# Modulation blocks and a bias moved from TensorE to VectorE, with reordered norm and final steps, in a two-layer hybrid diffusion step on eight cores

## The chip, the cores and the metric

The kernel runs on all 8 cores of one Trainium2 chip (two dies, cores 0 to 3 and 4 to 7). Each core runs the same program on its own share of the batch; the cores don't talk to each other. The metric is the device time of the slowest core, in microseconds, as the median of several runs.

## The reference

One step of a two-layer trunk, for context and latent tokens of width 1024. Each layer norms and modulates, mixes tokens, norms and modulates again, and runs an MLP with a squared ReLU:

```python
for l in range(DEPTH):                                   # 2 layers
    mod = (jax.nn.silu(cond) @ ada_w[l] + ada_b[l])[:, None, :]
    sh_m, sc_m, g_m, sh_f, sc_f, g_f = jnp.split(mod, N_MOD, axis=-1)
    h = rmsnorm(x, norm_mix_g[l]) * (1.0 + sc_m) + sh_m
    y = even_mixer(h, ...) if l % 2 == 0 else odd_mixer(h, ...)
    x = x + g_m * y
    h = rmsnorm(x, norm_ffn_g[l]) * (1.0 + sc_f) + sh_f
    x = x + g_f * (jnp.square(jax.nn.relu(h @ ffn_w1[l])) @ ffn_w2[l])
return rmsnorm(x, final_norm_g), outs_f, outs_b
```

`cond` is one vector for all context tokens and one per request for the latent tokens, so a core needs `mod` for two vectors. The even mixer is a chunked gated linear attention with a Fourier group; the odd one has a gated MLP over chunks of 128 positions and a short convolution:

```python
u, v = jnp.split(jax.nn.gelu(uv), 2, axis=-1)
sp = jnp.einsum('gpq,bnqgc->bnpgc', ws, vc) + bs.T[:, :, None]   # the gating bias
out_c = u * sp.reshape(bsz, L, GMLP_WIDTH)
out_d = gb * conv3(gc * hin, conv_w)
return jnp.concatenate([out_c, out_d], axis=-1) @ w_out
```

## The kernel before

**Tiles.** A core has 1536 tokens in three blocks `m` of 512, taken in the order MO = (2, 0, 1). Activations lie transposed: eight chunks of 128 channels in the partitions, tokens along the free axis. `xT[m]` holds the residual stream in f32, `hT` the modulated norm in bf16. A matmul group (`group`, L327) is 8 or 16 matmuls of 128x128 weights by 512 tokens into one PSUM bank; `PS()` (L285) hands out six banks in turn, and a second pair serves the sums of squares.

**Order of work.** Each engine runs its instructions in the order in which the program emits them; `Tracker.op` (L89) adds semaphore waits for the operands. Two lists mix work into the stream of groups. `defer` (L295) holds matmuls of the sums of squares, run some groups later by `pe_tick`. `side` holds the steps of a norm: `side_pop` (L313), called at the end of each `group`, emits `rate[0]` of them, before the consumer of that group's bank. `norm_steps` (L568) gives one step for the reciprocal root (Ln and Exp on ScalarE, into the one buffer `rstd`) and eight steps `ap(c)`: a product on VectorE into `ntm[c % 2]`, then at once the Identity with the shift on ScalarE that reads it. `norm_end` (L591) empties `side`, emits the root, and queues the steps; `need(m)` (L599) empties what is left before a block is read.

**Ada blocks.** `mod` is computed in twelve blocks of 1024 outputs. `ada_block` (L444) takes 64 weight loads of 128x128 with 64 matmuls of two columns, and one small addition on VectorE. Five run in the first half of the kernel; seven (`ada_next` in `ffn`) run in the MLP of layer 0, one after each w1 or w2 block of weights but the last.

**Weights.** Three slots of 2 MB (128 x 8192 bf16) take all weights in the order of `WSEQ`, in turn; `wpump` (L394) issues the next load on POOL's queue when its slot is free, and stops at the first that is not. `wdone` frees a slot.

**MLP** (`ffn`, L683). In each of two halves: two w1 blocks with 24 groups of eight matmuls (ReLU on ScalarE into one of two `relu_t`, square on VectorE), then two w2 blocks with 12 groups of sixteen matmuls (residual on VectorE, `resid` L606). In the last w2 block squares and norms run beside the groups; at the end of the kernel `final_steps` (L580) and `final_parts` (L632) do the last norm, for the last block of tokens in parts of 320 and 192 columns, and store the output.

**Gating** (`gmlp`, L1372). Per 128 tokens: one matmul of 33 rows by 512 columns puts the bias into the bank, four matmuls of 128 columns accumulate onto it, and VectorE multiplies with `uT`. Seven calls lie in the loop over the V groups, five in the output projection.

Helpers record their operations under one line each: L319 matmul, L333 activation, L336 tensor-tensor, L339 scalar-tensor-tensor (STT), L115 DMA.

Of the kernel before, what the change touches and what calls it, by code (L numbers as in the profile page):

```python
# [193 lines left out]
def build():  # L194
# [30 lines left out]
    with contextlib.ExitStack() as es:
# [25 lines left out]
        att = [sb("att%d" % i, [128, 512], BF16) for i in range(2)]  # L251
# [3 lines left out]
        relu_t = [sb("relu%d" % i, [128, 512], BF16) for i in range(2)]  # L255
# [99 lines left out]

        WSEQ = []
# [17 lines left out]
        for l in range(2):  # L374
# [3 lines left out]
            late = [(0, 5)] + [(1, k) for k in range(6)] if l == 0 else []  # L378
# [9 lines left out]
        wslot = [early[j] if j < len(early) else (2, 0, 1)[(j - len(early)) % 3] for j in range(len(WSEQ))]  # L388
        hw_b = Buf("hwslot")
        wstate = dict(issued=0, hold=len(early))  # L390
        wused = set()
        occ = [None] * NSLOT

        def wpump():  # L394
            while wstate["issued"] < min(len(WSEQ), wstate["hold"]):
                j = wstate["issued"]
                nm, n, src = WSEQ[j]
                sl = wslot[j]
                if occ[sl] is not None:
                    break  # L400
                occ[sl] = j
# [1088 lines left out]
```

How the kernel before makes its waits and increments, by code:

```python
    def _emit(self, e, need, fn):  # L71
        items = list(need.items())
        for key, (sem, val) in items[:-1]:
            e["h"].wait_ge(sem, val)
            e["seen"][key] = val
        ins = fn()
        if items:
            key, (sem, val) = items[-1]
            ins._wait_ge(sem, val)
            e["seen"][key] = val
        return ins
# [7 lines left out]
    def op(self, ek, fn, reads=(), writes=(), sig=True):  # L89
# [2 lines left out]
        e = self.eng[ek]  # L92
        need = self._collect(e, reads, writes)
        ins = self._emit(e, need, fn)
        if sig:
            e["cnt"] += 1
            ins.then_inc(e["sem"], 1)
            val = e["cnt"]
        else:
# [25 lines left out]
    def barrier(self, engines=("pe", "act", "dve", "sp")):  # L125
        if self.dead:
            return
        targets = [(k, e["sem"], e["cnt"]) for k, e in self.eng.items() if e["cnt"] > 0]
        targets += [("dma%d" % b.id, b.dsem, b.dcnt) for b in self.owners if b.dcnt > 0]
        for ek in engines:
            e = self.eng[ek]
            for key, sem, val in targets:
                if key == ek and ek == "pe":
                    continue
                if e["seen"].get(key, 0) >= val:
                    continue
                e["h"].wait_ge(sem, val)
                e["seen"][key] = val
# [1 line left out]
    def wait_all(self, ek, bufs):  # L140
        e = self.eng[ek]
        need = self._collect(e, [], bufs)
        for key, (sem, val) in need.items():
            e["h"].wait_ge(sem, val)
            e["seen"][key] = val
```

## Time and profile before

| | us |
|---|---|
| median of 3 runs | 1162.25 (1160.67 to 1163.19) |
| the profiled execution | 1162.37 |
| its span, slowest core (4) | 1161.1 |
| VectorE busy | 463.2 (40%) |
| ScalarE busy | 430.6 (37%) |
| POOL busy | 151.8 (13%) |

The span runs from the first to the last instruction of a core; the time of the execution has the launch on top. Busy time of TensorE overlaps itself, since matmuls are pipelined and their ends are modelled: one matmul of 512 columns is listed with 379 ns, while the starts of two in a row may lie closer. How fast TensorE goes is therefore read from start to start. A row of a timeline has its start, its duration from the first start to the last end, engine, line, operation, output and inputs, how many instructions are merged in it, and in brackets the idle time before it with what ended it.

### The profile page before, as it was taken

The page shows a single profiled execution, that of the slowest core. Times are in us where ns is not written, and L with a number is a line of the kernel's source. Part 1 is how long each engine was busy: PE and PEld are TensorE (multiplying, and loading weights), DVE is VectorE, ACT ScalarE, POOL GpSimd, SP SyncE. Part 2 cuts the span into 40 slices and gives each one's busy share as a digit, 9 for nine tenths or more (in the row PEclk, how much of TensorE's full clock was granted, in tenths as well). Part 3 has the DMA queues.
Part 4 walks back from the last instruction along what each step waited for, and adds up shares of the span by engine and source line. Part 5 has one row for each costly group of instructions (what it writes and reads, how often), then busy time and mean ns, then how long its engine had stood idle before and what let it go on. Part 6 is the DMA issues. An engine that isn't in the chain of part 4 may idle for free.

```text
span 1161.1 us, 16258 instructions; the slowest of 8 cores (1157.7 to 1161.1 us)
## 1 busy us (share of the span) xinstructions
PE 1094.6 (94%) x6519; PEld 547.6 (47%) x6519; DVE 463.2 (40%) x839; ACT 430.6 (37%) x823; POOL 151.8 (13%) x185
## 2 busy tenths in 40 slices
PE   2589999989999999999999999999999999999995
PEld 0234777755434444444444444444344444444444
DVE  2134588885642222222222637547432222222227
ACT  2275788856653200133202721227543000332032
POOL 1100223433400000000003300024000000000030
PEclk9998999999999999999999999999999999999999
DMA  9953747445367368458456224440440441240005
GB/s 183 215 120 63 124 79 167 87 153 115 64 113 123 68 101 127 73 91 133 69 90 109 36 37 73 73 73 1 73 73 5 69 73 28 46 73 1 1 1 218
DMA packets 14859, 99.27 MB, mean 85 GB/s; under 512 B 1578, under 2 KB 6858, under 8 KB 8768
## 3 DMA queue, kind: packets, MB, share of 16 engines
q0 software_dynamic: 6992, 81.07, 40.8%
q1 hardware_dynamic: 7248, 16.77, 4.4%
q8 instruction: 51, 0.84, 0.3%
q10 hardware_dynamic: 544, 0.39, 0.1%
q14 instruction: 24, 0.20, 0.1%
HBM read 164.88 MB, written 7.86 MB: 149 GB/s over the span
## 4 chain that ended last, share of the span: by engine, by line
PE 80%; ACT 8%; DVE 7%; DMA 3%; issue 2%; POOL 0%; ACTq 0%; DVEq 0%; POOLq 0%
PE psf L319 79%; DMA sb_slot<-evC 3%; DVE sb_ntm L339 2%; DVE sb_X L339 2%; ACT sb_hT L333 2%; ACT sb_relu L333 1%; ACT sb_A L333 1%; ACT sb_B L333 1%; DVE sb_A L336 1%; ACT sb_rstd L333 1%; ACT sb_lnr L333 1%; DVE sb_X L336 0%; PE psf L1058 0%; DVE sb_A L339 0%; ACT sb_X L347 0%
## 5 line engine op out<-in xcount | busy, mean ns | idle before, releaser
L319 PE MATMUL psf<-sb_hT,sb_slot 128*128 128x512 bf16 (+1 forms) x2472 | 557.9, 383 | 12.5 <-ACT sb_relu L333 4.9
L319 PEld LDWEIGHTS psf<-sb_hT,sb_slot 128*128 128x128 bf16 (+1 forms) x2472 | 240.1, 98 | 309.1 <-issue 15.0
L319 PE MATMUL psf<-sb_A,sb_slot 128*128 128x512 bf16 (+2 forms) x1696 | 359.4, 371 | 0.0
L319 PEld LDWEIGHTS psf<-sb_A,sb_slot 128*128 128x128 bf16 x1696 | 164.8, 98 | 186.8
L333 ACT ACTIVATE sb_relu<-psf 128x512 bf16<-128x512 f32 x192 | 113.6, 595 | 351.1 <-PE psf L319 350.0
L339 DVE SCALAR_TENSOR_TENSOR sb_X<-psf,sb_modT,sb_X 128x512 f32<-128x512 f32 (+2 forms) x148 | 108.4, 734 | 256.0 <-PE psf L319 255.9
L336 DVE TENSOR_TENSOR sb_A<-sb_relu 128x512 bf16<-128x512 bf16 x192 | 81.7, 425 | 237.4 <-ACT sb_relu L333 237.0
L333 ACT ACTIVATE sb_B<-sb_X 128x512 bf16<-128x512 f32 (+2 forms) x100 | 57.8, 607 | 155.0 <-DVE sb_X L339 145.7
L319 PE MATMUL psf<-sb_slot,sb_hT 128*128 128x192 bf16 (+2 forms) x672 | 90.5, 289 | 2.0 <-DVE sb_B L339 1.6
L508 POOL TENSOR_TENSOR sb_B<-sb_B 128x512 f32<-128x512 bf16 (+2 forms) x48 | 56.8, 1191 | 168.6 <-ACT sb_B L333 159.9
L333 ACT ACTIVATE sb_A<-psf 128x192 bf16<-128x192 f32 (+2 forms) x98 | 45.4, 466 | 78.3 <-PE psf L319 76.2
L319 PEld LDWEIGHTS psf<-sb_slot,sb_hT 128*128 128x128 bf16 x672 | 58.8, 98 | 26.1 <-ACT sb_A L333 1.3
L339 DVE SCALAR_TENSOR_TENSOR sb_ntm<-sb_X,sb_gscT,sb_rstd 128x512 f32<-128x512 f32 x72 | 58.7, 826 | 22.1 <-ACT sb_rstd L333 21.0
L333 ACT ACTIVATE sb_hT<-sb_ntm,sb_modT 128x512 bf16<-128x512 f32 x72 | 51.4, 721 | 38.3 <-DVE sb_ntm L339 38.0
L349 DVE CAST sb_A<-psf 128x512 bf16<-128x512 f32 (+1 forms) x33 | 22.2, 687 | 61.0 <-PE psf L319 61.0
L115 POOL DMA_DIRECT2D sb_slot<-w x16 | 8.6, 538 | 276.0 <-PE psf L319 276.0
L319 PE MATMUL psf<-sb_scT,sb_slot 128*128 128x2 bf16 x768 | 21.1, 163 | 21.0 <-DMA sb_slot<-adaw 21.0
L115 POOL DMA_DIRECT2D sb_slot<-adaw x12 | 6.6, 548 | 260.6 <-PE psf L319 260.6
L319 PE MATMUL psf<-sb_B,sb_onesb 128*128 128x512 bf16 (+2 forms) x53 | 19.1, 398 | 17.1 <-ACT sb_B L333 16.0
L319 PEld LDWEIGHTS psf<-sb_scT,sb_slot 128*128 128x128 bf16 x768 | 21.0, 97 | 23.3 <-DMA sb_slot<-adaw 21.6
L336 DVE TENSOR_TENSOR sb_X<-sb_X,sb_rstd 128x512 f32<-128x512 f32 (+1 forms) x30 | 19.1, 690 | 21.8 <-ACT sb_rstd L333 21.6
L508 POOL TENSOR_TENSOR sb_A<-sb_A 128x512 f32<-128x512 bf16 (+2 forms) x18 | 21.2, 1177 | 34.1 <-ACT sb_A L333 34.1
(125 smaller groups left out, 614.2 us busy)
## 6 DMA issues: line engine op xcount, KB each, us to landing
sb_slot<-w POOLq DMA_DIRECT2D x16, 2048.0 KB, 17.4
sb_slot<-adaw POOLq DMA_DIRECT2D x12, 2048.0 KB, 17.0
sb_X<-xT SPq DMA_DIRECT2D x6, 1024.0 KB, 10.3
sb_X<-xT POOLq DMA_DIRECT2D x4, 1024.0 KB, 29.1
yT<-sb_X SPq DMA_DIRECT2D x8, 512.0 KB, 3.3
sb_X<-xT POOLq DMA_DIRECT2D x4, 512.0 KB, 9.3
sb_slot<-evH POOLq DMA_DIRECT2D x1, 2048.0 KB, 16.7
sb_slot<-dft SPq DMA_DIRECT2D x1, 2048.0 KB, 17.2
```

The costliest lines, as they stand in the source:

```text
L115: ins = self._emit(e, need, lambda: e["h"].dma_start(out=out, in_=in_))
L319: T.op("pe", lambda: nc.tensor.matmul(out, l, r, start=start, stop=stop), reads=R, writes=W, sig=stop if sig is None else sig)
L333: T.op("act", lambda: nc.scalar.activation(out=out, in_=in_, func=func, **kw), reads=R, writes=W)
L336: T.op("dve", lambda: nc.vector.tensor_tensor(out=out, in0=a, in1=b, op=op), reads=R, writes=W)
L339: T.op("dve", lambda: nc.vector.scalar_tensor_tensor(out=out, in0=a, scalar=scalar, in1=b, op0=op0, op1=op1), reads=R, writes=W)
L349: T.op("dve", lambda: nc.vector.tensor_copy(out, in_), reads=R, writes=W)
L508: T.op("pool", lambda: nc.gpsimd.tensor_tensor(out=o[0], in0=a[0], in1=b[0], op=ALU.add), reads=[a[1], b[1]], writes=[o[1]])
```

## The change

Eight edits in one. Five ada blocks, (0,5), (1,0), (1,1), (1,2) in the MLP of layer 0 and (1,5) in that of layer 1, are computed on VectorE: the host lays their weights out with outputs in the partitions, the two Silu vectors are broadcast to all partitions (a load of 1 MB on SP's queue and two activations, in each MLP), and sixteen STT of 1024 columns with an accumulated sum give the block. A counter of units, one per w1 group and two per w2 group, places them: one per unit, from unit 17 + 28 i on. Blocks (1,3) and (1,4) stay on TensorE, later than before. The list of slots is written out by hand, and `wpump` no longer stops at a slot that is taken but goes on to loads for other slots. The norm's Identity of chunk c - 1 is emitted ahead of the product of chunk c, in nine steps for eight. In the final norm the roots of the later blocks go to `ntm[0]` and `ntm[1]` in place of `rstd`; in `final_parts` the side steps are emitted behind the residual and the square of a group, not ahead of them. The gating bias is computed once by a matmul, copied to SBUF in f32 (over `relu_t`), and added on VectorE, into `ntm`, before the product with `uT`.

```diff
+        ON_PE = ((1, 3), (1, 4))
+        LATE = ([(0, 5), (1, 0), (1, 1), (1, 2), (1, 3), (1, 4)], [(1, 5)])
...
-        wslot = [early[j] if j < len(early) else (2, 0, 1)[(j - len(early)) % 3] for j in range(len(WSEQ))]
+        wslot = list(early)
+        late_slots = [2, 0, 1, 0, 2, 0, 1, 0, 2, 0, 1, 0, 2, 1, 2, 1, 0, 2, 1, 2, 0, 1, 0, 1, 0, 1, 0]
+        wslot += late_slots[:len(WSEQ) - len(wslot)]
+        assert len(wslot) == len(WSEQ), (len(wslot), len(WSEQ))
...
         def wpump():
-            while wstate["issued"] < min(len(WSEQ), wstate["hold"]):
-                j = wstate["issued"]
+            blocked = set()
+            for j in range(min(len(WSEQ), wstate["hold"])):
+                sl = wslot[j]
+                if j in issued or sl in blocked:
+                    continue
+                if occ[sl] is not None:
+                    blocked.add(sl)
+                    continue
+                occ[sl] = j
                 nm, n, src = WSEQ[j]
...
+        def final_steps(m):
+            rf, rfb = (rstd, rstd_b) if m == MO[0] else (ntm[0], ntm_b[0])
+
+            def rs_():
+                ps, pb = sbank[m]
+                act(lnr[:], ps[:], AF.Ln, [pb, on_b], [lnr_b], bias=cst[:, 0:1])
+                act(rf[:], lnr[:], AF.Exp, [lnr_b], [rfb], scale=-0.5)
...
             def ap(c):
-                stt(ntm[c % 2][:], xT[m][:, c, :], gscT[l][:, wh, c, ci:ci + 1], rstd[:], ALU.mult, ALU.mult,
-                    [xT_b[m][c], rstd_b, gsc_b[l][wh]], [ntm_b[c % 2]])
-                act(hT[:, c, msl(m)], ntm[c % 2][:], AF.Identity, [ntm_b[c % 2], mod_b[l][shb]], [hT_b[m][c]],
-                    bias=modT[l][:, shb * 8 + c, ci:ci + 1])
-
...
+                if c > 0:
+                    act(hT[:, c - 1, msl(m)], ntm[(c - 1) % 2][:], AF.Identity, [ntm_b[(c - 1) % 2], mod_b[l][shb]], [hT_b[m][c - 1]],
+                        bias=modT[l][:, shb * 8 + c - 1, ci:ci + 1])
+                if c < 8:
+                    stt(ntm[c % 2][:], xT[m][:, c, :], gscT[l][:, wh, c, ci:ci + 1], rstd[:], ALU.mult, ALU.mult,
+                        [xT_b[m][c], rstd_b, gsc_b[l][wh]], [ntm_b[c % 2]])
+
+            return [lambda: rstd_calc(m)] + [lambda c=c: ap(c) for c in range(9)]
...
-                    act(rstd[:, hs], lnr[:, hs], AF.Exp, [st["l"]], [st["r"]], scale=-0.5)
+                    act(ntm[1][:, hs], lnr[:, hs], AF.Exp, [st["l"]], [st["r"]], scale=-0.5)
...
-                rate[0] = 2 + hh
+                rate[0] = 0
...
                     qdefer(1, s_, fn)
+                    side_pop(2 + hh)
...
+        def sc_rows(olds):
+            stg = B[:, 0:4096].bitcast(F32)
+            sb_ = ab("stg", olds)
+            T.dma("sp", stg, condb_d, Buf("condb"), writes=[sb_])
+            sc = ab("scB", att_b + olds)
+
+            def silu(k):
+                act(scB[k], stg[:, k * 1024:(k + 1) * 1024], AF.Silu, [sb_], [sc])
...
+        def ada_rows(l, b, sc, jk):
+            st = {}
+
+            def one(oc, k):
+                if not st:
+                    st["s"], st["b"] = wget("ada%d_%d" % (l, b))
+                w = st["s"][:, oc * 1024:(oc + 1) * 1024]
+                T.op("dve", lambda: nc.vector.scalar_tensor_tensor(out=B[:, 1024 * k:1024 * (k + 1)], in0=w, scalar=1.0, in1=scB[k],
+                                                                   op0=ALU.mult, op1=ALU.mult, accum_out=mraw[:, oc, k:k + 1]),
+                     reads=[st["b"], sc], writes=[jk[k], mraw_b])
+                if oc == 7 and k == 1:
+                    wdone(st["b"])
+                    mod_add(l, b, mraw[:], mraw_b)
+
+            return [lambda oc=oc, k=k: one(oc, k) for oc in range(8) for k in range(2)]
...
+            sc, jk, silu = sc_rows(B_all)
+            B_all.extend([sc] + jk)
+            rows = {14: [lambda: silu(0), lambda: silu(1)]}
+            for i, (la, ba_) in enumerate([x for x in LATE[l] if x not in ON_PE]):
+                for k_, fn in enumerate(ada_rows(la, ba_, sc, jk)):
+                    rows.setdefault(17 + 28 * i + k_, []).append(fn)
+            late = [x for x in LATE[l] if x in ON_PE]
+            un = [0]
+
+            def unit(n):
+                for _ in range(n):
+                    for fn in rows.get(un[0], []):
+                        fn()
+                    un[0] += 1
 
...
                             tt(aT[:, ch, msl(m)], relu_t[i][:], relu_t[i][:], ALU.mult, [relu_b[i]], [aT_b[ch][m]])
+                            unit(1)
                     wdone(slb)
-                    ada_next()
+                    if hf == 1 and b == 1 and late:
+                        ada_block(*late.pop(0))
...
                             resid(l, 5, oc, m, ps, pb)
+                            unit(2)
...
-                    if not last:
-                        ada_next()
+                    if pre and late:
+                        ada_block(*late.pop(0))
...
+        biasf = relu_all[:].bitcast(F32)
+        bias_b = ab("bias", relu_b)
+        ps, pb = PS()
+        mm(ps[:], ones33[:], gb33[:], [on_b, gb_b], [pb])
+        cp(biasf, ps[:], [pb], [bias_b], "dve")
...
-            mm(ps[:], ones33[:], gb33[:], [on_b, gb_b], [pb], start=True, stop=False)
             for g in range(4):
-                mm(ps[:, g * 128:(g + 1) * 128], v1[:, j, g * 128:(g + 1) * 128], wsT(g), [v1_b[j], wst_b], [pb],
-                   start=False, stop=(g == 3))
-            tt(hT[:, 0:4, tsl(j)], ps[:].rearrange("p (g t) -> p g t", g=4), uT[:, :, tsl(j)], ALU.mult,
-               [pb] + [u_b[c][m] for c in range(4)], [hT_b[m][c] for c in range(4)])
+                mm(ps[:, g * 128:(g + 1) * 128], v1[:, j, g * 128:(g + 1) * 128], wsT(g), [v1_b[j], wst_b], [pb], sig=(g == 3))
+            nt, ntb = ntm[j % 2], ntm_b[j % 2]
+            tt(nt[:], ps[:], biasf, ALU.add, [pb, bias_b], [ntb])
+            tt(hT[:, 0:4, tsl(j)], nt[:].rearrange("p (g t) -> p g t", g=4), uT[:, :, tsl(j)], ALU.mult,
+               [ntb] + [u_b[c][m] for c in range(4)], [hT_b[m][c] for c in range(4)])
```

On the host, `adaw` keeps its old layout for the seven blocks that stay on TensorE and is transposed for the five others; `condb` is the pair of conditioning vectors, repeated over 128 partitions. `mod_add` is the addition at the end of `ada_block`, made a function.

## Rows read from the trace of the kernel before

**Rows 1.** The cores: span, mean granted clock of TensorE.

```profile
core 0: 1157.8 us, clock 0.993
...
core 4: 1161.1 us, clock 0.991
```

**Rows 2.** Busy time, share of the span and instructions, from the page.

```profile
PE 1094.6 (94%) x6519; PEld 547.6 (47%) x6519; DVE 463.2 (40%) x839; ACT 430.6 (37%) x823; POOL 151.8 (13%) x185
```

**Rows 3.** Timeline of the first MLP's first groups, 317 to 340 us.

```profile
317.70 9.23 PE L319 MATMUL psf<-sb_hT,sb_slot 128*128 128x512 bf16 x42
...
327.24 1.90 PE L319 MATMUL psf<-sb_hT,sb_slot 128*128 128x512 bf16 x8 [0.31 <-ACT sb_relu L333]
...
329.92 0.75 DVE L339 SCALAR_TENSOR_TENSOR sb_ntm<-sb_X,sb_gscT,sb_rstd 128x512 f32<-128x512 f32 x1
330.70 0.72 ACT L333 ACTIVATE sb_hT<-sb_ntm,sb_modT 128x512 bf16<-128x512 f32 x1 [1.16 <-DVE sb_ntm L339]
331.33 0.58 ACT L333 ACTIVATE sb_relu<-psf 128x512 bf16<-128x512 f32 x1
331.94 0.42 DVE L336 TENSOR_TENSOR sb_A<-sb_relu 128x512 bf16<-128x512 bf16 x1 [1.27 <-ACT sb_relu L333]
...
339.04 13.99 PE L319 MATMUL psf<-sb_hT,sb_slot 128*128 128x512 bf16 x64 [0.46 <-ACT sb_relu L333]
```

**Rows 4.** Timeline of the second MLP's first groups, TensorE, 819 to 842 us.

```profile
819.73 11.90 PE L319 MATMUL psf<-sb_hT,sb_slot 128*128 128x512 bf16 x53
...
832.09 1.90 PE L319 MATMUL psf<-sb_hT,sb_slot 128*128 128x512 bf16 x8 [0.46 <-ACT sb_relu L333]
...
841.53 1.69 PE L319 MATMUL psf<-sb_hT,sb_slot 128*128 128x512 bf16 x7 [0.46 <-ACT sb_relu L333]
```

**Rows 5.** Timeline of TensorE around one ada block, 352 to 355 us.

```profile
352.86 1.74 PE L319 MATMUL psf<-sb_scT,sb_slot 128*128 128x2 bf16 x64
...
354.46 3.83 PE L319 MATMUL psf<-sb_hT,sb_slot 128*128 128x512 bf16 x17
```

**Rows 6.** Timeline of TensorE in the V loop with gating, 749 to 753 us.

```profile
749.67 0.39 PE L319 MATMUL psf<-sb_gb,sb_ones 33*128 33x512 bf16 x1
...
749.99 0.40 PE L319 MATMUL psf<-sb_cb,sb_A 128*128 128x128 bf16 x4
...
750.23 1.89 PE L319 MATMUL psf<-sb_slot,sb_hT 128*128 128x512 bf16 x8
...
752.05 0.39 PE L319 MATMUL psf<-sb_gb,sb_ones 33*128 33x512 bf16 x1
```

**Rows 7.** VectorE by shape: busy us, mean ns of one, idle before.

```profile
L339 DVE SCALAR_TENSOR_TENSOR sb_X<-psf,sb_modT,sb_X 128x512 f32<-128x512 f32 x140 | 104.6, 749 | 255.9 <-PE psf L319 255.9
...
L339 DVE SCALAR_TENSOR_TENSOR sb_A<-sb_B,sb_pp,sb_A 128x1008 f32<-128x1008 f32 x8 | 10.1, 1268 | 0.3
```

**Rows 8.** ScalarE by shape, same columns.

```profile
L333 ACT ACT_TABLE_LOAD x10 | 12.8, 1283 | 15.2 <-PE psf L319 14.0 <-PEq L195 1.1
...
L333 ACT ACTIVATION_READ_ACCUMULATOR sb_A<-psf 128x1 f32 x48 | 9.4, 196 | 0.0
```

**Rows 9.** The tail from 1129 us: TensorE's waits (us, times, longest), then timeline.

```profile
PE psf L319 <- ACT sb_B L333: 3.8, 3, 1.5
...
1138.27 0.63 ACT L333 ACTIVATE sb_rstd<-sb_lnr 128x512 f32<-128x512 f32 x1 [1.23 <-DVE sb_X L339]
...
1153.92 2.72 DVE L339 SCALAR_TENSOR_TENSOR sb_X<-sb_X,sb_pp,sb_rstd 128x192 f32<-128x192 f32 x8 [1.59 <-ACT sb_rstd L333]
```

**Rows 10.** The loads of ada blocks, twelve of 2 MB, from issue to landing.

```profile
DMA to landing us min/median/max: 16.4/17.0/34.2
```

**Rows 11.** Windows of core 4: TensorE busy (instructions), granted clock, DMA share, GB/s.

```profile
290.00:295.00 5.00, 5.00 (x20) 0.81 0.96 177
...
850.00:1130.00 280.00, 280.00 (x1299) 1.00 0.22 38
```

More of the change, by code:

```diff
@@ L250, in build @@
         lnr_b = Buf("lnr")
-        att = [sb("att%d" % i, [128, 512], BF16) for i in range(2)]
+        att_all = sb("att", [128, 1024], BF16)
+        att = [att_all[:, i * 512:(i + 1) * 512] for i in range(2)]
+        mraw = sb("mraw", [128, 8, 2])
         att_b = [Buf("att0"), Buf("att1")]
@@ L254, in build @@
         ntm_b = [Buf("ntm0"), Buf("ntm1")]
-        relu_t = [sb("relu%d" % i, [128, 512], BF16) for i in range(2)]
+        relu_all = sb("relu", [128, 1024], BF16)
+        relu_t = [relu_all[:, i * 512:(i + 1) * 512] for i in range(2)]
         relu_b = [Buf("relu0"), Buf("relu1")]
@@ L377, in build @@
                 wadd("odUV", 8192, odUV_d); wadd("odO", 8192, odO_d)
-            late = [(0, 5)] + [(1, k) for k in range(6)] if l == 0 else []
+            late = LATE[l][:]
             for hf in range(2):
@@ L405, in wpump @@
                     T.dma("pool", slots[sl][:, 0:n], src, slot_b[sl], writes=[slot_b[sl]])
-                wstate["issued"] += 1
+                issued.add(j)
+                blocked.add(sl)
         def wget(name):
             j = [i for i in range(len(WSEQ)) if WSEQ[i][0] == name and i not in wused][0]
-            assert wstate["issued"] > j, name
+            assert j in issued, name
             wused.add(j)
@@ L681, in final_parts @@
                 side.pop(0)()
+        scB = [att_all[:], B[:, 7168:8192]]
+        mraw_b = Buf("mraw")
+        def sc_rows(olds):
[5 more added lines that the diff above has]
+                act(scB[k], stg[:, k * 1024:(k + 1) * 1024], AF.Silu, [sb_], [sc])
+                if k == 1:
+                    for j in jk:
+                        for dct in (sb_.w, sb_.r):
+                            for key, (sem, val) in dct.items():
+                                Tracker._rec(j.r, key, sem, val)
+            jk = [ab("jk", olds) for _ in range(2)]
+            return sc, jk, silu
+        def ada_rows(l, b, sc, jk):
[11 more added lines that the diff above has]
+            return [lambda oc=oc, k=k: one(oc, k) for oc in range(8) for k in range(2)]
         def ffn(l, nxt):
@@ L688, in ffn @@
             k = [0]
-            late = [(0, 5)] + [(1, k) for k in range(6)] if l == 0 else []
-            def ada_next():
-                if late:
-                    ada_block(*late.pop(0))
+            sc, jk, silu = sc_rows(B_all)
[11 more added lines that the diff above has]
+                    un[0] += 1
             rate[0] = 1
@@ L1401, in build @@
                     gmlp(rest.pop(0))
+        for b in relu_b:
+            for dct in (bias_b.w, bias_b.r):
+                for key, (sem, val) in dct.items():
+                    Tracker._rec(b.r, key, sem, val)
         ffn(1, "final")
```

38 lines of the change are left out of this document (20 added, 18 removed).

## Prediction

> **What bounds the kernel now.** I read the spans of all cores first: core 4 takes 1161.1 us, core 0 takes 1157.8 us, and the granted clock is 0.991 and 0.993 [rows 1]. The slowest core sets the time, so all the work below is on core 4. The share of busy time names TensorE: 1094.6 us of the span [rows 2]. Busy is not yet bound, so I looked at the pitch. Between 339.04 and 352.86 us TensorE starts 64 matmuls of 512 columns, 13.82 us or 0.216 us each [rows 3, 5]; one group of eight is 1.73 us. Most of both MLPs runs at that pitch, so there an instruction less on TensorE is time less, and VectorE and ScalarE have room. The exceptions are found in the chain of waits, which leaves TensorE in the norm before either MLP and again in the last 30 us; the timelines of those stretches show where.
>
> First exception: in the first MLP, groups start 2.36 us apart ((339.04 - 327.24) / 5) [rows 3]. The rows between show the ring: VectorE's norm product (0.75 us), ScalarE's Identity that waits for it, ScalarE's ReLU queued behind that Identity, and VectorE's square that waits for the ReLU and stands ahead of the next product [rows 3]. Together they take 2.36 us where TensorE needs 1.73. Second exception: at the end TensorE waits 3.8 us for ScalarE's squares, and VectorE's queue is full of final products [rows 9].
>
> **Ada blocks.** Five of twelve blocks leave TensorE. One block delays the next group from 352.86 to 354.46 us: 1.60 us [rows 5], although its weight loads and matmuls number 64 each. Five: **8.0 us**. (Its modelled busy time, 1.74 us, would give 8.7; I take the pitch.)
>
> What they add to VectorE: 16 products of 128x1024 per block, each with an accumulated sum. No row shows that form. The nearest is the 128x1008 product at 1.27 us [rows 7]; ScalarE's accumulator read is a separate 0.20 us [rows 8]. So I take 1.45 us. The lower end is 0.6 us (two products of 512 would run 1.5 us, and two bf16 elements per cycle, as the square seems to do at 0.42 us [rows 3] against 0.75, would halve that); the upper end is twice the row, 2.5 us. They are spread one to a unit, a unit being one w1 group or half a w2 group. In a w1 unit VectorE then has 0.42 + 1.45 = 1.87 us against 1.73: it falls behind by 0.14 us a unit, 2.2 us over 16 units, and has 12 empty units after each block to catch up. The cover is the ring of six PSUM banks: TensorE may run five groups ahead, 5 x 1.73 = 8.6 us, before VectorE's lag reaches it through the ReLU. In w2 groups it is 0.75 [rows 7] + 2.90 = 3.65 us against 3.45, with twice the cover. Cost nothing, as long as the cover holds; it fails in w1 units from 16 x (0.42 + x - 1.73) = 8.6, that is x = 1.85 us. Behind a waiting product on VectorE stand the square, and behind it ReLU and the bank.
>
> Each of the two MLPs also gets a 1 MB load of the conditioning rows on SP's queue (nothing needed soon is behind it; it shares the engines with a weight load when TensorE has its weights already), two Silu of 1024 columns and a table load at unit 14. A 512-column Identity is 0.72 us [rows 3], so two Silu are at most 2.9 us, with 1.28 us for the table [rows 8]: 4.2 us, against 8.6 us of cover and after the norm is through. Going back to Ln costs 1.28 us once more in each final norm; in the second MLP that lies on the tail and is counted there.
>
> **Slots.** A slot is now held through 16 units, and weights are loaded by slot, not in one order. The tightest pair is the second block: its load can start when the first is read out (unit 33, some 2 us late) and it is needed at unit 45, 12 x 1.73 = 20.7 us later; landing takes 17.0 us in the middle and 34.2 at worst [rows 10]. Cover: the same 8.6 us. The w1 and w2 weights keep 24 units, 41 us. On POOL's queue each load waits behind nothing later than itself. Cost nothing.
>
> **Gating bias.** One turn of the V loop takes 752.05 - 749.67 = 2.38 us; its V group is 1.73 and its four gating matmuls 750.23 - 749.99 = 0.24 [rows 6]. The bias matmul with its weight load thus costs 0.41 us, more than its 0.216 us of columns. Twelve go, one comes: 11 x 0.41 = **4.5 us** (by columns alone 2.4, the lower end; 4.9 the upper). VectorE gets 12 additions and a copy of 0.7 us, against 1.97 us of TensorE per turn: hidden.
>
> **Norm skew.** With the Identity of c - 1 ahead of the product of c, ScalarE never waits for the product just issued. VectorE then has 0.75 + 0.42 and ScalarE 0.72 + 0.60 us per group, both under 1.73. In the first MLP the 42 matmuls from 317.70 should have ended at 326.8, and the next start at 327.24 is 0.5 us late; five turns lose 0.63 each: 3.7 us [rows 3]. In the second, 53 matmuls from 819.73 end at 831.2, the next starts at 832.09 (0.9 late), four turns follow to 841.53 and lose 2.5: 3.5 us [rows 4]. Together **7.2 us**, if the stall goes wholly; the upper end is that, the lower zero. The flush before the last rstd remains, some 4 us of lag on ScalarE (three Identities and rstd) which the banks cover.
>
> **Tail.** Residuals come ahead of the final products, and the Exp no longer waits for the old products (1.23 us at 1138.27) [rows 9]. But VectorE's own work fills most of the tail, and the 8 products of 192 columns after the last rstd stay (2.72 us from 1153.92) [rows 9], so at most the 3.8 us of TensorE's waits come back; the table load (1.28 us) may come on top. I take **1.5 us**, between -1.3 and 3.8.
>
> **Sum.** 8.0 + 4.5 + 7.2 + 1.5 = 21.2 us. The profiled execution took 1162.4 us (span and launch), 0.1 above the median: 1162.4 - 21.2 - 0.1 = **1141.1 us**.
>
> **Rivals.** (1) The norm stall stays in another form, with the extra step of ten instead of nine before need() or with the flush: 1141.1 + 7.2 = 1148.3. For it: the flush puts three steps and both root activations on ScalarE at once. Against: both engines have 0.4 us to spare per group.
> (2) VectorE's accumulating product is dearer, 2.0 us: each of the three blocks in w1 units (two in the first MLP, one in the second) stalls TensorE by 16 x 0.69 - 8.6 = 2.4 us: 7.3 in all, 1148.4.
> (3) **Slower**: the product costs double, 2.5 us. Then each of the three w1 blocks stalls 16 x 1.19 - 8.6 = 10.4 us and the w2 blocks 1 us each, 33 us in all: 1174. It turns slower than before from x = 2.29 us, where 3 x (16 x (x - 1.31) - 8.6) passes 21. Against it: the product with two f32 operands from SBUF runs 0.75 us, just as the one with a PSUM operand [rows 3, 7].
> The Trainium skill (Vector Engine (DVE) Microarchitecture Reference, section 7, Points that are easy to get wrong) says that a scalar-tensor-tensor with two non-bf16 SBUF sources halves throughput for want of a port for the accumulator. The trace shows no halving without an accumulator, and the new sources are bf16, so by its own words the rule spares this change; were it to hold here, it would be this rival.
> (4) The clock: with fewer gaps the granted clock falls. It was 0.81 for 5 us at 290 us on core 4, and 1.00 (2.4 GHz) through 850 to 1130 us where TensorE had no gap at all [rows 11]. At 0.81 the 21 us are used up after some 90 us. One sentence of the Trainium skill bears on it: TensorE: Matmul & The Clock Gate, Part 1, has the whole die fall to 13/16 once three cores run dense matmuls, for as long as they do; eight cores ran dense for 280 us here without it, so the trace disagrees.
> (5) The edits do not do what they say: the blocks moved are on TensorE's path by the row, so only a misplaced slot could undo them; I give it nothing of its own.
>
> **Chances.** Forecast 0.76; (1) 0.09; (2) 0.08; (3) 0.04; (4) 0.03. A measurement tells 0.2% (2.3 us) from no change. All but (3) and (4) are faster by more: 0.93, and of the rest 0.02 the same and 0.05 slower. The range: best ends 8.7 + 4.9 + 7.2 + 3.8 = 24.6 give 1137.6, and the 1.5 us that core 4 lost to the clock dip may be absent, 1136; at the top it takes in (1) and (2), 1150.
>
> **What would show it.** The idle-before of ReLU-bound matmuls gone at 325 and 830 us; groups 1.73 us apart through both; 448 instead of 768 ada matmuls; VectorE's new rows near 1.45 us and no PE wait behind them; V turns at 1.97 us; a tail of 2 us less. What would make it wrong: the new products over 1.85 us, a DMA wait on VectorE over 8 us, or a clock below 1.00 in the MLPs.

## The result, and the profile after

The changed kernel takes 1145.43 us (median; 1143.69 to 1146.15) where the kernel before, run beside it, takes 1161.83 us: a ratio of 0.9854, with an interval of 0.9837 to 0.9871. That is 16.4 us less by the medians (17.0 by the ratio), inside the range of the prediction (1136 to 1150) and 4.3 us above its point. Now and then one die runs slow for a long stretch of an execution (one of the four of the changed kernel took 1245.22 us, with one die at a mean clock of 0.90, and with the mended tail below it went down to 0.81); such executions are left out of the ranges and ratios but not of the medians, which puts 1145.43 where 1144.9 would stand and moves no other median given below by more than 0.4 us. In a second comparison on another chip, told below, the same kernel takes 1140.67 us against 1160.23.

The spans of all cores come first. These are those of the profiled execution of the changed kernel (1146.15 us):

```profile
core 3: 1144.7 us, clock 0.986
core 4: 1138.5 us, clock 0.993
...
die 0 (median of its cores): 1143.7 us, clock 0.988
die 1 (median of its cores): 1138.5 us, clock 0.993
```

The program is the same on all cores, yet one die is 5.2 us longer, at a lower clock. The windows of core 3 show where (TensorE busy, weight loads, VectorE, ScalarE, POOL, granted clock, DMA share, GB/s):

```profile
290.00:300.00 10.00, 10.00 (x42) 4.23 (x40) 8.25 (x12) 6.43 (x11) 4.68 (x4) 0.86 1.05 203
...
760.00:770.00 10.00, 10.00 (x50) 4.62 (x49) 7.10 (x12) 3.15 (x5) 5.20 (x5) 0.91 0.65 109
810.00:820.00 10.00, 10.00 (x43) 4.28 (x42) 5.90 (x12) 6.88 (x12) 0.00 (x0) 0.88 0.89 159
850.00:1130.00 280.00, 279.33 (x1342) 130.50 (x1341) 80.27 (x143) 57.53 (x97) 16.52 (x17) 1.00 0.27 52
```

The clock sags for ten microseconds at a time at several places and is 1.00 on the mean from 850 us on. It is the same kind of dip as in [rows 11], only more of them. To see what the edits did I therefore compare cores without a dip: core 0 of before (1157.8 us, clock 0.993 [rows 1]) and core 4 of after (1138.5 us, 0.993). The starts of the 192 ReLUs of both MLPs cut either span into stretches:

| stretch | before | after | difference |
|---|---|---|---|
| start to the first ReLU | 308.86 | 308.94 | +0.1 |
| MLP of layer 0, first 48 w1 groups | 84.99 | 80.07 | -4.9 |
| its w2 groups | 89.41 | 84.60 | -4.8 |
| next 48 w1 groups | 82.75 | 81.16 | -1.6 |
| last w2 groups and the odd mixer | 244.51 | 239.78 | -4.7 |
| MLP of layer 1, first 48 w1 groups | 83.32 | 80.19 | -3.1 |
| its w2 and w1 groups | 165.76 | 165.75 | 0.0 |
| last ReLU to the end | 98.2 | 98.0 | -0.2 |
| span | 1157.8 | 1138.5 | -19.3 |

The page after, beside [rows 2]: VectorE has 100.6 us more work, TensorE 331 matmuls less, five blocks of 64 and 11 for the bias.

```profile
PE 1083.2 (95%) x6188; PEld 541.0 (47%) x6188; DVE 563.8 (49%) x1012; ACT 437.2 (38%) x831; POOL 153.2 (13%) x185
```

The first MLP on TensorE, core 4, beside [rows 3], and then the second, beside [rows 4]. The columns are start, duration, engine, line, operation, output and inputs, how many:

```profile
310.99 34.26 PE L323 MATMUL psf<-sb_hT,sb_slot 128*128 128x512 bf16 x158
```

```profile
799.74 45.49 PE L323 MATMUL psf<-sb_hT,sb_slot 128*128 128x512 bf16 x210
```

Each is one unbroken row, where before there were gaps that ended with a ReLU. The timeline of core 4 shows the conditioning rows being made, and then the units with an accumulating product:

```profile
332.64 1.28 ACT L337 ACT_TABLE_LOAD   x1
...
333.94 1.06 ACT L337 ACTIVATE sb_att<-sb_B 128x1024 bf16<-128x1024 f32 x1
335.02 1.06 ACT L337 ACTIVATE sb_B<-sb_B 128x1024 bf16<-128x1024 f32 x1
...
339.56 0.42 DVE L340 TENSOR_TENSOR sb_A<-sb_relu 128x512 bf16<-128x512 bf16 x1
339.90 1.22 DVE L738 SCALAR_TENSOR_TENSOR sb_B<-sb_slot,sb_B 128x1024 bf16<-128x1024 bf16 x1
...
341.05 0.08 DVE L738 DVE_READ_ACCUMULATOR sb_B<-sb_slot,sb_B 128x1 f32 x1
341.29 0.43 DVE L340 TENSOR_TENSOR sb_A<-sb_relu 128x512 bf16<-128x512 bf16 x1 [0.16 <-ACT sb_relu L337]
```

From the square at 339.56 to the end of the accumulator's read at 341.13 VectorE needs 1.57 us, and then it idles 0.16 us for the next ReLU: a unit costs less than the group's 1.73. By shape (busy us, mean ns of one, idle before), core 4, with ScalarE's table loads under it:

```profile
L738 DVE SCALAR_TENSOR_TENSOR sb_B<-sb_slot,sb_att 128x1024 bf16<-128x1024 bf16 x40 | 48.8, 1220 | 0.5
L738 DVE SCALAR_TENSOR_TENSOR sb_B<-sb_slot,sb_B 128x1024 bf16<-128x1024 bf16 x40 | 48.7, 1217 | 0.0
...
L337 ACT ACT_TABLE_LOAD x14 | 18.0, 1283 | 15.2 <-PE psf L323 14.0 <-PEq L195 1.1
```

The V loop with gating on TensorE, core 4, beside [rows 6]:

```profile
741.62 0.39 PE L323 MATMUL psf<-sb_cb,sb_A 128*128 128x128 bf16 x4
741.84 1.89 PE L323 MATMUL psf<-sb_slot,sb_hT 128*128 128x512 bf16 x8
743.57 0.39 PE L323 MATMUL psf<-sb_cb,sb_A 128*128 128x128 bf16 x4
```

A turn is 743.57 - 741.62 = 1.95 us, where it was 2.38. And the tail, core 4, beside [rows 9]:

```profile
1112.92 0.55 DVE L343 SCALAR_TENSOR_TENSOR sb_X<-psf,sb_modT,sb_X 128x320 f32<-128x320 f32 x1 [1.36 <-PE psf L323]
...
1113.38 3.92 DVE L343 SCALAR_TENSOR_TENSOR sb_X<-sb_X,sb_pp,sb_rstd 128x512 f32<-128x512 f32 x5
...
1117.22 0.54 DVE L343 SCALAR_TENSOR_TENSOR sb_X<-psf,sb_modT,sb_X 128x320 f32<-128x320 f32 x1
...
1126.22 1.01 DVE L343 SCALAR_TENSOR_TENSOR sb_X<-sb_X,sb_pp,sb_ntm 128x320 f32<-128x320 f32 x2 [1.46 <-ACT sb_ntm L337]
1127.15 0.41 DVE L343 SCALAR_TENSOR_TENSOR sb_X<-psf,sb_modT,sb_X 128x192 f32<-128x192 f32 x1
...
1130.87 2.72 DVE L343 SCALAR_TENSOR_TENSOR sb_X<-sb_X,sb_pp,sb_ntm 128x192 f32<-128x192 f32 x8 [0.21 <-ACT sb_ntm L337]
```

VectorE idles 1.36 us at 1111.56, with five old products at hand that it is only given at 1113.38; these hold the next residual back until 1117.22. Near the end it waits 1.46 us for the second root, and the residual at 1127.15 stands behind the two products that need that root. The order of the tail is new, and its work is a little shorter: the last eight products start 20.33 us after the first 320-column part (1110.54), where that was 21.01. Of these 0.7 us the table shows only 0.2, because the span goes on for 4.9 us behind the last product (which ends at 1133.59), where that was 4.4; only stores and semaphore instructions lie there.

### The profile page after: what moved, and what is told of

Its sections match the earlier page's. It is cut to its first block, busy times and chain, and to the rows that moved or that the text cites. A ratio compares the mean times of both kernels' runs of the same rounds, so it can differ in the third digit from the quotient of the medians.

```text
span 1144.7 us, 15757 instructions; the slowest of 8 cores (1137.1 to 1144.7 us)
## 1 busy us (share of the span) xinstructions
PE 1083.2 (95%) x6188; PEld 541.0 (47%) x6188; DVE 563.8 (49%) x1012; ACT 437.2 (38%) x831; POOL 153.2 (13%) x185
## 4 chain that ended last, share of the span: by engine, by line
PE 86%; ACT 5%; DVE 4%; DMA 3%; issue 1%; POOL 0%; ACTq 0%; DVEq 0%; POOLq 0%
PE psf L323 85%; DMA sb_slot<-evC 3%; DVE sb_X L343 2%; ACT sb_B L337 1%; ACT sb_A L337 1%; ACT sb_hT L337 1%; DVE sb_A L340 0%; ACT sb_lnr L337 0%; DVE sb_X L340 0%; PE psf L1134 0%; ACT sb_rstd L337 0%; DVE sb_A L343 0%; DVE sb_ntm L343 0%; ACT sb_X L351 0%; ACT L337 0%
## 5 line engine op out<-in xcount | busy, mean ns | idle before, releaser
L738 DVE SCALAR_TENSOR_TENSOR sb_B<-sb_slot,sb_att 128x1024 bf16<-128x1024 bf16 x40 | 48.8, 1220 | 0.5
L738 DVE SCALAR_TENSOR_TENSOR sb_B<-sb_slot,sb_B 128x1024 bf16<-128x1024 bf16 x40 | 48.7, 1217 | 0.0
L323 PE MATMUL psf<-sb_B,sb_onesb 128*128 128x512 bf16 (+2 forms) x53 | 19.3, 403 | 15.9 <-ACT sb_B L337 15.0
L323 PE MATMUL psf<-sb_scT,sb_slot 128*128 128x2 bf16 x448 | 12.4, 164 | 22.3 <-DMA sb_slot<-adaw 22.3
L526 POOL TENSOR_TENSOR sb_A<-sb_A 128x512 f32<-128x512 bf16 (+2 forms) x18 | 21.2, 1176 | 33.8 <-ACT sb_A L337 33.8
```

Of the source, the lines that this page charges most:

```text
L323: T.op("pe", lambda: nc.tensor.matmul(out, l, r, start=start, stop=stop), reads=R, writes=W, sig=stop if sig is None else sig)
L526: T.op("pool", lambda: nc.gpsimd.tensor_tensor(out=o[0], in0=a[0], in1=b[0], op=ALU.add), reads=[a[1], b[1]], writes=[o[1]])
L738: T.op("dve", lambda: nc.vector.scalar_tensor_tensor(out=B[:, 1024 * k:1024 * (k + 1)], in0=w, scalar=1.0, in1=scB[k], op0=ALU.mult, op1=A ...
```

## The experiments

**The four parts alone.** Four kernels each have one part of the change, all else as before, run on one chip beside the kernel before (1159.78 us).

Only the ada blocks with their slots and `wpump`:

```diff
+        ON_PE = ((1, 3), (1, 4))
+        LATE = ([(0, 5), (1, 0), (1, 1), (1, 2), (1, 3), (1, 4)], [(1, 5)])
+            sc, jk, silu = sc_rows(B_all)
```

> Kernel before with the ada edit alone: five blocks on VectorE, the new list of slots, the loads by slot; norm order, tail and bias as before. Theory (work leaves TensorE's path at its pitch): each core 8.0 us (5 x 1.60) shorter than the kernel before on an undisturbed die, the norm stall of 2.36 us per group still there before both MLPs. Rival (the moved work costs something on VectorE or through the slots): less than 6 us. On the clock: if the denser matmul stream makes the clock dip, the dips on the disturbed die grow here by 1 to 2 us; if the norm order does it, they stay as in the kernel before.

Measured: 1152.41 us, 7.4 less, ratio 0.9939 (0.9923 to 0.9955). The ReLU stall of [rows 3] is still there; TensorE's waits, core 4 (us, times, longest):

```profile
PE psf L323 <- ACT sb_relu L337: 4.9, 11, 0.5
```

The stretches hold the full 8.0 us (first w1 groups 84.99 to 83.38, w2 groups 89.41 to 84.61, next w1 groups 82.75 to 81.15). But from the last ReLU to the end it is 98.6 us on all cores for 98.2, although the tail is untouched: the last product ends where it did, and the part behind it is 0.4 us longer. Why is open.

Only the skewed norm steps:

```diff
+                if c > 0:
+                    act(hT[:, c - 1, msl(m)], ntm[(c - 1) % 2][:], AF.Identity, [ntm_b[(c - 1) % 2], mod_b[l][shb]], [hT_b[m][c - 1]],
+                        bias=modT[l][:, shb * 8 + c - 1, ci:ci + 1])
...
+            return [lambda: rstd_calc(m)] + [lambda c=c: ap(c) for c in range(9)]
```

> Kernel before with the norm order alone (Identity of chunk c - 1 ahead of the product of chunk c). Theory: TensorE's waits for ReLU before both MLPs vanish, 6.4 us shorter (3.3 in the first MLP, 3.1 in the second, as the milestones of the changed kernel give), groups 1.73 us apart throughout. Rival: part of the 6.4 us came from the other edits and less than 4 us is seen here. On the clock: if taking gaps from TensorE in stretches with all engines busy brings dips, the disturbed die gives 2 us or more of it back.

Measured: 1152.57 us, 7.2 less, ratio 0.9943 (0.9925 to 0.9961). No wait of TensorE for a ReLU is left. On core 0 the first 48 w1 groups go from 84.99 to 81.66 us, 3.3 less, those of layer 1 from 83.32 to 80.19, 3.1 less, and the stretch with the odd mixer from 244.51 to 244.18.

Only the gating bias on VectorE:

```diff
+        cp(biasf, ps[:], [pb], [bias_b], "dve")
...
+            tt(nt[:], ps[:], biasf, ALU.add, [pb, bias_b], [ntb])
```

> Kernel before with the gating bias on VectorE alone. Theory: the bias matmul with its exposed weight load costs 0.41 us a turn, so 4.5 us shorter (4.7 by the milestones of the changed kernel). Rival (a bias matmul costs only its 512 columns, 0.216 us): 2.4 us.

Measured: 1155.75 us, 4.0 less, ratio 0.9965 (0.9952 to 0.9978). On core 4 the stretch with the odd mixer goes from 244.51 to 239.83 us, 4.7 less, as in the whole change.

Only the tail:

```diff
-                rate[0] = 2 + hh
+                rate[0] = 0
...
+                    side_pop(2 + hh)
```

> Kernel before with the tail edit alone: own root buffers, residual and square ahead of the side steps in the last parts. The changed kernel's last ReLU to its end took 98.0 us against 98.2 before, so the forecast 1.5 us was not there. Theory 1 (the edit itself gives nothing, because VectorE idles 1.4 us at the first part and the root of part one comes 1 us later): 0 to 0.7 us shorter here too. Theory 2 (the edit gives 1.5 us and the table load of 1.28 us took it back): 1.3 to 1.5 us shorter here, where no table load lies ahead of the last norm.

Measured: 1159.03 us, 0.75 less, ratio 0.9991 (0.9981 to 1.0001): by the times no difference that can be told from none. The traces do tell one: from the last ReLU to the end it is 97.4 to 97.5 us on all eight cores, where it was 98.2.

The four add up: 7.4 + 7.2 + 4.0 + 0.75 = 19.4 us.

**The changed kernel again**, unaltered, on another chip beside before (1160.23 us). The question is whether the longer die of the first comparison belongs to the program.

> The changed kernel itself, once more. The four parts alone gave 7.4, 7.2, 4.0 and 0.8 us, 19.4 in sum. Theory 1 (the parts add up; the 3 us that were missing in the first comparison are clock dips of one die, which belong to the execution): 19 us shorter here if both dies are undisturbed, with all cores alike within 2 us and the clock near 0.993. Theory 2 (the four together load the chip so that one die's clock dips more than with any part alone): cores of one die 4 to 6 us longer than the other again, at 0.987 or so, and 15 to 16 us shorter in all.

Measured: 1140.67 us, 19.6 less, ratio 0.983 (0.982 to 0.9841). The dies of its profiled execution:

```profile
die 0 (median of its cores): 1138.5 us, clock 0.993
die 1 (median of its cores): 1138.3 us, clock 0.992
```

Both are as core 4 was in the first comparison. The parts lose nothing when they are put together (19.4 against 19.6), and the 5 us of one die are the clock's in those executions: the same program runs without them here. The chip of the first comparison was not tried again, so whether the dips belong to that chip or to that series was not found out.

**The tail mended.** In the final norm the old steps are no longer emptied at once, the root is emitted without waiting for a turn, and two products go ahead of the first part's first residual, where VectorE idled.

```diff
-            while side:
+            while side and nxt != "final":
...
-                side.append(rs_)
+                rs_()
...
+                    if hh == 0 and o == 0:
+                        side_pop(2)
...
-                    side_pop(2 + hh)
+                    side_pop(2)
```

> The changed kernel with another tail: the old steps of the final norm are no longer emptied ahead of the next root, the root of each last part is emitted at once and not through the side list, two side steps go ahead of the first part's residual, and two instead of three behind each residual of the second. Theory (VectorE's idle time of 1.4 us at the first part and of 1.5 us before each late root is what the tail edit left): last ReLU to end falls from 98.0 to about 96 us, 2 us shorter than the changed kernel. Rival (the tail is set by TensorE's own groups and the last chain of residual, square, sum, root and products): under 0.5 us.

Measured: ratio to before 0.9816 (0.9792 to 0.984); two executions, 1138.28 and 1139.43 us. The dies are at 1136.3 and 1136.5 us, 2.0 less than in the run above, but only 1.3 of it lies in the tail: on core 4 the last ReLU to the end falls from 98.0 to 96.7 us, where about 96 was expected. Of TensorE's 3.2 us of waits for ScalarE in the tail this is left on core 4:

```profile
PE psf L323 <- ACT sb_B L337: 0.6, 1, 0.6
```

So the tail held some 1.3 us that the change didn't take. Which of the four edits gives how much of it was not taken apart.

**A sixth block.** On top of the mended tail, block (1,3) goes to VectorE too, the blocks 27 units apart instead of 28 so that all five of layer 0's MLP are read out before its last w1 group, unit 143.

```diff
-        ON_PE = ((1, 3), (1, 4))
+        ON_PE = ((1, 4),)
-                    rows.setdefault(17 + 28 * i + k_, []).append(fn)
+                    rows.setdefault(17 + 27 * i + k_, []).append(fn)
```

> The kernel with the other tail, and a sixth ada block, (1,3), on VectorE in the MLP of layer 0, with blocks 27 units apart in place of 28. Theory (each block is worth 1.60 us of TensorE's pitch while VectorE keeps up): 1.6 us shorter than with five. Rival (the load of the next block has 11 units, 19 us, against a landing of 18, and VectorE's wait for it reaches TensorE): no gain or a loss, with TensorE waiting for ReLU.

Measured: 1137.55 us, ratio 0.9804 (0.9787 to 0.9821). The stretch that holds block (1,3) goes from 239.79 (the mended tail) to 238.18 us: 1.6, the price of a block once more. The dies:

```profile
die 0 (median of its cores): 1135.0 us, clock 0.993
die 1 (median of its cores): 1134.4 us, clock 0.992
```

The loop of loads told of below has 27 x 1.73 = 46.7 us here. This is the fastest version of the study, 3.1 us under the changed kernel by the medians of one chip.

**The accumulating product twice.** This measures the cover: what TensorE feels once VectorE falls behind.

```diff
+                for _ in range(2):
+                    T.op("dve", lambda: nc.vector.scalar_tensor_tensor(out=B[:, 1024 * k:1024 * (k + 1)], in0=w, scalar=1.0, in1=scB[k],
+                                                                       op0=ALU.mult, op1=ALU.mult, accum_out=mraw[:, oc, k:k + 1]),
+                         reads=[st["b"], sc], writes=[jk[k], mraw_b])
```

> The changed kernel with each accumulating product issued twice, so that a unit has 2.6 us of it (measured 1.22 + 0.08 each). This puts rival 3 of the prediction to the test. By its formula each of the three blocks in w1 units stalls TensorE by 16 x (0.42 + 2.6 - 1.73) - 8.6 = 12.0 us and the two in w2 units by 8 x (0.75 + 5.2 - 3.45) - 17.2 = 2.8 us: 42 us longer than the changed kernel, 22 us longer than the kernel before. If the banks cover more than five groups (two ReLU buffers on top), 6 to 10 us less than that. If VectorE's lag is hidden otherwise, no change.

Measured: 1191.75 us, ratio 1.027 (1.0245 to 1.0294): 51 us over the changed kernel, 9 more than expected. VectorE in the first block, core 0:

```profile
352.43 0.42 DVE L340 TENSOR_TENSOR sb_A<-sb_relu 128x512 bf16<-128x512 bf16 x1
...
354.03 1.23 DVE L739 SCALAR_TENSOR_TENSOR sb_B<-sb_slot,sb_att 128x1024 bf16<-128x1024 bf16 x1
...
355.18 0.42 DVE L340 TENSOR_TENSOR sb_A<-sb_relu 128x512 bf16<-128x512 bf16 x1
```

A unit is 2.75 us, so over 16 units VectorE falls 16 x (2.75 - 1.73) = 16.4 us behind. The first 48 w1 groups on core 0 grow from 80.06 to 86.65 us, by 6.6; the second MLP's by the same (86.73 against 80.19). The cover is thus 16.4 - 6.6 = 9.8 us. But the other stretches grow more: the w2 groups by 10.8 and the next w1 groups by 21.9 us (103.05 against 81.15), and there VectorE waits for its weights:

```profile
DVE sb_B L739 <- DMA sb_slot<-adaw: 21.4, 3, 10.8
```

The load of the next block waits for the read-out of the last, and the one behind it on POOL's queue waits along (TensorE did not wait for that one here). POOL, core 0:

```profile
440.07 0.53 POOL L115 DMA_DIRECT2D sb_slot<-adaw  x1 [45.73 <-DVE sb_modT L340]
440.58 0.54 POOL L115 DMA_DIRECT2D sb_slot<-w  x1
```

**One short product more.** A product of 512 columns is added to each accumulating one (its result isn't used). This is rival (2) made real.

```diff
+                stt(B[:, 1024 * k:1024 * k + 512], w[:, 0:512], 1.0, scB[k][:, 0:512], ALU.mult, ALU.mult, [st["b"], sc], [jk[k]])
```

> The changed kernel with one more product of 512 columns beside each accumulating product (its result is not used), so that a unit has about 2.0 us of them: rival 2 of the prediction. By the prediction's formula each of the three blocks in w1 units stalls TensorE by 16 x (0.42 + 2.0 - 1.73) - 8.6 = 2.4 us, 7.3 us in all. Theory from the run with doubled products: there the pitch of VectorE was 2.75 us a unit, 16.4 us of lag over the first block, and TensorE lost 6.6 us, so the cover is 9.8 us; here the pitch is about 2.1 us, 6 us of lag, all of it covered: no change against the changed kernel (within 0.5 us).

Measured: 1148.61 us in the middle of three executions (1147.86 to 1150.11), ratio to before 0.9899 (0.9878 to 0.992), 8 us over the changed kernel. The cores fall into two groups:

```profile
core 0: 1138.4 us, clock 0.993
core 1: 1147.8 us, clock 0.991
...
core 3: 1148.7 us, clock 0.993
```

A unit now takes VectorE 2.21 us on either core (squares at 346.70 and 348.91 us on core 0), 0.48 more than a group, or 7.7 us behind per block, inside the cover of 9.8. And on both the first 48 w1 groups take what they took, 80.06 and 80.07 us. The 9 us between the cores come later: in the next w1 groups core 1 takes 88.87 us and core 0 81.33. The issues of the ada loads on POOL, core 0 and then core 1:

```profile
373.58 0.53 POOL L115 DMA_DIRECT2D sb_slot<-adaw  x1 [25.33 <-DVE sb_modT L340]
423.22 0.53 POOL L115 DMA_DIRECT2D sb_slot<-adaw  x1 [33.53 <-DVE sb_modT L340]
472.14 0.53 POOL L115 DMA_DIRECT2D sb_slot<-adaw  x1 [41.01 <-DVE sb_modT L340]
520.88 0.53 POOL L115 DMA_DIRECT2D sb_slot<-adaw  x1 [47.69 <-DVE sb_modT L340]
```

```profile
375.19 0.53 POOL L115 DMA_DIRECT2D sb_slot<-adaw  x1 [25.33 <-DVE sb_modT L340]
426.14 0.53 POOL L115 DMA_DIRECT2D sb_slot<-adaw  x1 [34.85 <-DVE sb_modT L340]
477.74 0.53 POOL L115 DMA_DIRECT2D sb_slot<-adaw  x1 [45.01 <-DVE sb_modT L340]
530.03 0.53 POOL L115 DMA_DIRECT2D sb_slot<-adaw  x1 [51.23 <-DVE sb_modT L340]
```

And the landings of all twelve ada loads, core 0 and then core 1:

```profile
DMA to landing us min/median/max: 12.6/14.9/34.3
```

```profile
DMA to landing us min/median/max: 15.3/17.0/35.3
```

The issues are 49.6, 48.9 and 48.7 us apart on core 0, and 51.0, 51.6 and 52.3 us on core 1. The blocks are placed 28 units apart, 28 x 1.73 = 48.4 us. But a block's load can only be issued when the block before is read out, then it must land, and then it is read out in 16 units: a closed loop. The read-out takes 16 x 2.21 = 35.4 us. The loads behind the first three issues shown land after 14.0, 13.3 and 13.3 us on core 0 and after 15.3, 16.0 and 16.9 us on core 1, so the loop should take 49.4, 48.7 and 48.7 us on core 0 and 50.7, 51.4 and 52.3 on core 1: the distances of the issues to within 0.3 us. Where the loop is longer than the 48.4 us, each turn puts VectorE further behind, and the cover is spent once, not given anew to each block. On core 1 VectorE waits for these loads:

```profile
DVE sb_B L343 <- DMA sb_slot<-adaw: 17.8, 3, 9.5
```

On core 0 it waits 5.2 us for them. The other cores go the same way: on four of the eight the ada loads land after 14.9 to 16.4 us in the median, and the next w1 groups take 81.3 to 83.0 us; on the other four it is 16.9 to 17.3 us, and they take 88.9 to 91.3.

The doubled kernel fits: 17.0 + 16 x 2.75 = 61.0 us, and on its core 1 the issues are 60.9, 62.3 and 60.7 us apart. In the changed kernel the loop takes 17.0 + 16 x 1.73 = 44.7 us, with 3.7 us to spare. Why an ada load lands 2 us sooner on some cores is open. In each of the three executions one core of each pair of neighbours (0 and 1, 2 and 3, 4 and 5, 6 and 7) is short, 1137 to 1141 us, and the other long, 1146 to 1149 us; which of the two it is changes between executions, so neither the core's data nor its place decides it.

**The doubled kernel with its blocks 36 units apart**, so that the loop (61.0 us) fits into 36 x 1.73 = 62.3.

```diff
-                    rows.setdefault(17 + 28 * i + k_, []).append(fn)
+                    rows.setdefault(17 + 36 * i + k_, []).append(fn)
```

> The changed kernel with doubled products, blocks 36 units apart in place of 28. Theory (of the 51 us that doubling cost at 28 units, VectorE's lag against the banks makes 6.6 us for each block in w1 units, and the rest comes from loads that start late because the slot is read out late, with VectorE waiting 21 us for them): with 8 more units between blocks those waits go, and the cost falls from 51 to 15 to 25 us over the changed kernel. Rival (all of it is VectorE's own work against the cover, slots play no part): it stays above 40 us.

Measured: 1194.02 us, ratio 1.0293 (1.0277 to 1.031): no gain, where 15 to 25 us were expected. VectorE no longer waits for an ada load on core 0, where that was 21.4 us. But the fourth block is now read out about where the w1 groups end, and the slot that it holds is the one that block (1,3) needs, which runs on TensorE right behind them. TensorE, core 0:

```profile
559.63 7.93 PE L323 MATMUL psf<-sb_hT,sb_slot 128*128 128x512 bf16 x34
...
595.65 1.84 PE L323 MATMUL psf<-sb_scT,sb_slot 128*128 128x2 bf16 x64 [28.09 <-DMA sb_slot<-adaw]
```

Its load is issued at 581.43 us. The wait moved from VectorE to TensorE, by my placing of the blocks. The w2 groups, 10.8 us longer in the doubled kernel, are 1.4 us longer here (86.04 us against 84.61, core 0), with 23 units of products among them for 29. So this run confirms that the spacing takes the loop's wait from VectorE; the forecast of the total failed, and what the total would be without a late load is not shown.

## Why the prediction came out as it did

**What bounds.** Right: work taken from TensorE in the MLPs and the V loop came back as time, one for one, on all the cores that no dip disturbed.

**Ada blocks, 8.0 us.** Right: three blocks less in the w2 stretch give 4.8 us, one in the next w1 stretch 1.6, one in the first w1 stretch 1.6 (84.99 to 83.38 in the kernel with this edit alone), and the sixth block 1.6. That kernel gained 7.4 and not 8.0 us; 0.4 of the difference is the longer end behind the last product, a term that the prediction doesn't have. The pitch of [rows 5] was the right row, not the busy time. The product was taken at 1.45 us and costs 1.23 (339.90 to 341.13), with its accumulator's read at 0.08 us against ScalarE's 0.20 [rows 8]. Thus VectorE doesn't fall behind by 0.14 us a unit but has 0.16 to spare. The cover of 8.6 us measured 9.8. The two Silu of 1024 columns take 2.1 us and the table 1.3, under the bound of 4.2, and TensorE shows no gap there.

**Slots, nothing.** Right in this kernel, but the reasoning had a hole that the runs with a dearer product laid open. I put the pair's 20.7 us against a landing of 17.0 and then gave it "the same 8.6 us" of cover, as if each pair began anew. The loads form a loop: lag adds up from turn to turn. The loop breaks at a unit of (48.4 - 17.0) / 16 = 1.96 us (at 2.19 with the 13.3 us of core 0, which a unit of 2.21 hardly hurt), the banks of a single block only at 1.73 + 9.8 / 16 = 2.34 us. The threshold in the prediction, 1.85 us a product or 2.27 a unit, stood for the banks alone; the loads come first. "On POOL's queue each load waits behind nothing later than itself" also failed: once VectorE is late, a weight load is queued behind the ada load that waits for VectorE (440.07 us above).

**Gating bias, 4.5 us.** Right, 4.7: a turn is 1.95 us where 1.97 was forecast, 11 x 0.43.

**Norm skew, 7.2 us.** The stall is gone in both MLPs, and it gave 3.3 and 3.1 us, 6.4 in all; 0.8 was too much. The term is that of the first row of each stretch, 0.5 and 0.9 us of lateness, worked out from a count of merged matmuls; the rest of the working, turns of 0.63 us, would have given 3.15 and 2.5. Alone, this part gave 7.2 us by the medians of another chip; its stretches hold 6.8 of them, 0.3 with the odd mixer, which the whole change doesn't show (239.78 us, and 239.83 with the bias edit alone). Rival (1) is out.

**Tail, 1.5 us.** This is the term that was mis-sized the most: 0.75 us alone (0.7 to 0.8 by the traces of all cores), and 0.2 us in the stretch table, where the longer end behind the last product takes 0.5 back. Its sign, its bounds and the cause that I named against it (VectorE full of its own products, and the eight last ones) hold: only 0.6 of TensorE's 3.8 us of waits went, 3.2 stayed. Another order gave 1.3 us more. The table load that I set against the tail cost the last norm 0.1 us: ScalarE does it at 1105.24 us while it waits for the sums of squares, and the first Ln lies 4.0 us ahead of the first 320-column part, before 4.1.

**Sum.** 8.0 + 4.7 + 6.4 + 0.2 = 19.3 us against a forecast of 21.2. From the before of the second comparison, 1160.23, the forecast would be 1139.0, and the run gave 1140.67. The rest of the distance in the first comparison (1145.43 us) is the clock of one die. I had named a fallen clock as rival (4) and a mended one in the range, but as a whole-kernel effect and as 1.5 us; in the event dips of a few microseconds cost one die 5.2 us after and 3.3 before (1161.1 against 1157.8 [rows 1]), and the metric takes the slower die. A clock below 1.00 in the MLPs, which I had named as a sign of being wrong, was there on core 3: the first w1 groups of the two MLPs take 0.9 and 1.1 us more than on core 4, and the rest of the 6.2 us between these cores lies outside them. That the point came out only 4.3 us off in spite of this is in part luck: the kernel before, from which I started, had dips too (1161.83 us against 1160.23 in the second comparison).

**Rivals (2) and (3).** (2), at a product of 2.0 us, forecast a stall of the three w1 blocks by the banks, 1148.4. The run built for it came to 1148.61, the forecast number by another way: no stall by the banks, 8 us by the loads, on half of the cores. That the two numbers agree is luck. (3), a product of 2.5 us: the doubled kernel is slower than before by 2.7%, 51 us over the changed kernel; 6.6 of these come by the banks in the first stretch of either MLP, and the stretches in which VectorE also waits for loads hold 32.7 on core 0. The Trainium skill (Vector Engine (DVE) Microarchitecture Reference, section 7) says that two SBUF sources that are not bf16 halve the throughput of a scalar-tensor-tensor. No run here tests that with an accumulated sum: these sources are bf16, and 1024 columns of them take 1.22 us.

## What to carry to other kernels

Before work is moved to an engine beside the bound one, work out two thresholds, not one: how long the mover may lag until the ring of buffers is full, and how long one turn of its operand loop is (read-out, load, landing) against the turn that the schedule gives it; the second can break first, and it adds up. Price a moved block by the pitch of starts on the bound engine, and test the cover by a kernel in which the moved work is made dearer. In a tail where the second engine is full, a new order of its work gains little (here 0.7 us): look for its idle time (here 1.36 us) and put old work there.

## What the runs showed of the hardware that was not expected

- A scalar-tensor-tensor of 128x1024 in bf16 with an accumulated sum takes 1.22 us and 0.08 us for the accumulator's read, about as much as the 128x1008 one in f32 without a sum (1.27 us [rows 7]). A product of 128x512 in bf16 without a sum takes 0.69 us (in the kernel with the short product), against 0.75 in f32: bf16 buys little in this form.
- The granted clock dipped to between 0.86 and 0.94 in single windows of 10 us on core 3 that show 1.00 on core 4 of the other die. It cost that die 5.2 us in one comparison and nothing in the next. In the kernel with 36 units, where TensorE stood still for 28 us, it was at 0.50 (1.2 GHz) between 572 and 598 us, and in the doubled one between 490 and 500 us, where TensorE was busy for 6.15 of 10 us. No rule can be read from this: from 470 to 480 us, with 6.40 us busy, it was 1.00 on the same core (0):

```profile
490.00:500.00 10.00, 6.15 (x14) 2.08 (x16) 9.79 (x19) 0.60 (x1) 0.13 (x1) 0.50 0.00 0
```

- Cores that run the same program can lie 9 us apart at nearly the same clock (1138.4 us at 0.993 and 1147.8 us at 0.991 with the short product) once a loop of loads is near its limit: an ada load lands in 14.9 us on one and in 17.0 us on the other. Of two neighbours one was short and one long in every execution of that kernel, in changing roles.
